# Inverse row sums of attention: written wide by VectorE and turned by four transposes a pair, in place of eight products of the identity

## The reference, cut to what matters

```python
p = exp(s - row_max(s))            # 512 x 512
o = (p @ v) / p.sum(axis=-1)       # 512 x 64: every row of o times the inverse of its row sum
```

## Time and profile before

| | |
|---|---|
| time before, median of 3 runs | 3227.48 us (3226.89 to 3227.84) |
| span of the profiled execution | 3226.3 us |
| its own time | not given apart from the span; the median of the runs is 1.2 us above the span, which is taken as what lies around it |
| TensorE products busy | 3183.2 us (99%) |
| VectorE busy | 1879.4 us (58%) |
| ScalarE, GpSimd busy | 512.8 us (16%), 231.0 us (7%) |
| attention of layer 1, 2621.80 to 2762.20 us: busy TensorE, VectorE, ScalarE | 129.89, 99.93, 82.37 us of 140.40 us |

### The profile page before, as it was taken

One profiled execution on the slowest core, in us unless ns is written; L12 is line 12 of the kernel. 1 busy time (PEld: TensorE's weight loads), 2 busy tenths in 40 slices (PEclk: granted clock), 3 DMA queues, 4 the chain that ended last, 5 costly groups with the idle time before them and its releaser, 6 DMA issues.

```text
span 3226.3 us, 36432 instructions
## 1 busy us (share of the span) xinstructions
PE 3183.2 (99%) x14382; PEld 2591.5 (80%) x14382; DVE 1879.4 (58%) x3268; ACT 512.8 (16%) x1080; POOL 231.0 (7%) x206
## 2 busy tenths in 40 slices
PE   9999999999999999999999999999999999999999
PEld 3888758888888888884488888888888854788888
DVE  6356845764347764464776664466644647766643
ACT  2111122000011000105521000110001145210001
POOL 1244400000000000003000000000000030000000
PEclk9999999999999999999999999999999999999999
DMA  5254321222222222223012222222222230122221
GB/s 237 89 173 161 135 70 53 92 80 90 92 82 92 82 85 85 90 72 124 1 64 81 92 86 88 89 83 87 88 85 88 74 124 1 53 92 88 82 84 61
DMA packets 43882, 288.31 MB, mean 89 GB/s; under 512 B 5404, under 2 KB 5404, under 8 KB 12736
## 3 DMA queue, kind: packets, MB, share of 16 engines
q1 hardware_dynamic: 39024, 271.14, 24.2%
q0 software_dynamic: 4688, 14.85, 1.4%
HBM read 281.76 MB, written 2.11 MB: 88 GB/s over the span
## 4 chain that ended last, share of the span: by engine, by line
PE 91%; DVE 5%; DVEq 1%; ACT 1%; issue 1%; DMA 0%; ACTq 0%; POOL 0%
PE ps L831 76%; PE ps L550 3%; PE ps L1274 2%; PE ps L966 1%; PE ps L1242 1%; PE ps L1185 1%; DVE arena L1888 1%; PE ps L531 1%; PE ps L858 1%; PE ps L931 1%; DVE arena L2310 1%; ACT arena L1586 1%; PE ps L1256 1%; DVEq L2323 1%; PE ps L1281 0%
## 5 line engine op out<-in xcount | busy, mean ns | idle before, releaser
L831 PE MATMUL ps<-arena 128*128 128x256 f32 x5456 | 1244.9, 379 | 0.1
L831 PEld LDWEIGHTS ps<-arena 128*128 128x128 f32 x5456 | 1036.6, 190 | 141.5 <-DVE arena L2061 0.5
L831 PE MATMUL ps<-arena,ring 128*128 128x256 f32 x2768 | 646.1, 379 | 0.5 <-ACT arena L1314 0.5
L831 PEld LDWEIGHTS ps<-arena,ring 128*128 128x128 f32 x2768 | 525.7, 190 | 72.4 <-ACT arena L1314 0.9
L831 PE MATMUL ps<-xn,ring 128*128 128x256 f32 x2272 | 518.8, 379 | 5.8 <-DVE arena L1704 2.3
L831 PEld LDWEIGHTS ps<-xn,ring 128*128 128x128 f32 x2272 | 431.2, 190 | 71.9 <-issue 9.4
L1698 DVE TENSOR_TENSOR arena<-arena,ps 128x512 f32<-128x512 f32 x173 | 118.9, 687 | 553.3 <-PE ps L831 494.4
L1671 DVE TENSOR_TENSOR arena<-ring 128x512 f32<-128x512 f32 (+1 forms) x194 | 131.1, 676 | 347.5 <-PE ps L831 347.3
L831 PE MATMUL ps<-xn,arena 128*128 128x256 f32 x1264 | 302.2, 379 | 0.0
L831 PEld LDWEIGHTS ps<-xn,arena 128*128 128x128 f32 x1264 | 240.2, 190 | 32.6
L1502 ACT ACTIVATE arena<-arena 128x512 f32<-128x512 f32 x88 | 55.4, 630 | 883.3 <-DVE arena L2180 883.3
(11 more groups left out here) (321 smaller groups left out, 2510.9 us busy)
## 6 DMA issues: line engine op xcount, KB each, us to landing
ring<-in_w_up_a SPq DMA_DIRECT2D x44, 1024.0 KB, 4.9
ring<-in_w_up_b SPq DMA_DIRECT2D x44, 1024.0 KB, 4.9
ring<-in_w_ff SPq DMA_DIRECT2D x32, 1024.0 KB, 4.9
ring<-in_w_ada SPq DMA_DIRECT2D x24, 1024.0 KB, 5.0
ring<-in_w_down_a SPq DMA_DIRECT2D x16, 1024.0 KB, 4.9
ring<-in_w_down_b SPq DMA_DIRECT2D x16, 1024.0 KB, 4.9
ring<-in_w_in SPq DMA_DIRECT2D x14, 1024.0 KB, 4.9
ring<-in_w_out SPq DMA_DIRECT2D x12, 1024.0 KB, 5.3
```

The lines of the kernel that those rows point to most:

```text
L831: mm = nc.tensor.matmul(out_ap, w, operand(product, quads[i]), start=at not in opened, stop=last_chunk and i == len(quads) - 1, skip_group ...
```

## The change

VectorE now follows the reciprocal with a drain (the copy reads what the reciprocal wrote) and a copy that repeats each of the eight inverses 64 times: `inv_wide`, 128 partitions x 512, in one of the two halves of a scratch buffer that is unused during attention. The semaphore `inverted` is raised by the copy. On TensorE the eight products with the identity (two passes each, 64 of the array's columns) become four 128 x 128 transposes of `inv_wide`, each giving the rows of both heads for one tile of queries.

```diff
+        inv_wide = square_of
...
                     for i in range(ST):
-                        for u in range(2):
-                            mm = nc.tensor.matmul(turn_bank((layer, "norm", j))[64 * u:64 * u + 64, i * P:(i + 1) * P],
-                                                  inv_p[:, j % 2, u, i:i + 1].to_broadcast([P, 64]), ident,
-                                                  start=True, stop=True)
+                        mm = nc.tensor.transpose(turn_bank((layer, "norm", j))[:, i * P:(i + 1) * P],
+                                                 inv_wide[:, j % 2, i * P:(i + 1) * P], ident)
                     mm.then_inc(sem("turned"), 1)
...
                 def invert(j, n):
                     dve.wait_ge(sem("exps"), UNITS_2 * layer + 2 * n + 2)
-                    nc.vector.reciprocal(inv_p[:, j % 2, :, :], sums_p[:, j % 2, :, :]).then_inc(sem("inverted"), 1)
+                    nc.vector.reciprocal(inv_p[:, j % 2, :, :], sums_p[:, j % 2, :, :])
+                    dve.drain()
+                    every = inv_p[:, j % 2, :, :].rearrange("p u (i o) -> p i u o", o=1).to_broadcast([P, ST, 2, 64])
+                    wide_to = inv_wide[:, j % 2, :].rearrange("p (i u w) -> p i u w", i=ST, u=2)
+                    nc.vector.tensor_copy(wide_to, every).then_inc(sem("inverted"), 1)
```

## The result

The changed kernel takes 3231.88 us (median of 21 runs, 3229.80 to 3233.37) against 3227.85 us for the kernel before (21 runs, 3226.75 to 3229.68): 4.0 us more, a ratio of 1.0013 with a 95% interval from 1.0007 to 1.0018. That is slower, by less than the 0.2% that was set as no change; the forecast was 3227.8, the range 3224.0 to 3233.0. So 1.9 us lie around a span, not the 1.2 taken before; the sum goes by differences, so that it does not enter.

A forecast was written before the change was run, and what follows sets the result against it. TensorE was taken to set the pace in long blocks, VectorE for some microseconds behind each. TensorE's -5.3 and VectorE's +5.6 gave +0.3 us on 3227.5, so 3227.8 us, range 3224.0 to 3233.0.

The forecast's parts named there:

- rival 1: VectorE's wide copy goes number by number because of its repeated source: +3.4 us, 3230.9 us; chance 0.22.
- rival 4: VectorE's wide copy waits for a full GpSimd add over shared SBUF ports: 7.4 us in all, 3235.2; chance 0.05.
- TensorE: what is removed and added: Transposes replacing identity products in attention save 2.63 us a layer, 5.3 in all, after paying for changes of tiling.
- A rule against the change: Skill's rule that TensorE transposes miss the full clock: new blocks 7.0 us longer in all, 3234.8; chance 0.02.
- VectorE: what is added: Drain and wide copy behind each reciprocal on VectorE add 0.49 us an invert, at the far end 0.75.
- What hides it: VectorE idle time hides the layer's first and last inverts; the others cost 2.81 us a layer, both 5.6.
- Rival 3: Longer VectorE work shifts TensorE's clock falls from C steps into B steps: two falls give 3234.6 us; chance 0.07.
- Rival 2: VectorE's additions behind the five on-chain reciprocals find cover: half covered 3225.0 us, all covered 3222.2; chance 0.12.

The follow-up runs named there:

- e1: Kernel before with only TensorE's side changed: four transposes of scratch data, no wide copy, so the turned numbers are not the inverses; 3221.33 us, ratio 0.9979.
- e3: Changed kernel with only the invert of each layer's first pair moved three steps later on VectorE's queue; 3228.89 us, ratio 1.0003 against the kernel before.
- e6: Changed kernel with the first pair's copy made a product reading one tile from SBUF, one from PSUM (that pair's result scaled wrongly); 3228.55 us, ratio 1.0003.
- e4: Changed kernel with all inverts but each layer's last moved three steps later on VectorE's queue; 3222.38 us, ratio 0.9983 against the kernel before.
- e2: Kernel before with only VectorE's side changed: drain and wide copy behind every reciprocal, identity products kept; 3236.60 us, ratio 1.0028.
- e5: Changed kernel run again, unedited, for a second trace; 3232.08 us, ratio 1.0014 against the kernel before.

## Why the prediction was right or wrong

The time lay in the upper part of the range, and within 0.2% as forecast; the sum missed by 3.7 us (+4.0 against +0.3). That it lay in the range is luck in part: the upper part was there for rival 1 and a fall of the clock, neither of which set the time. What did, rival 4, had been put beyond the range, at 3235.2. One sign of being right failed: the attention stretches were to keep their length within 1 us, and grew by 2.20 and 0.55 in the first trace, by 2.00 and 2.16 in the second.

- *TensorE: what is removed and added.* Right. Forecast 2.63 a layer; e1 has 2.68 and 2.62. Both halves of the price of a changed tiling, read from neighbouring rows, were there: 3.58 against 3.48 on leaving, 0.50 against 0.44 on arriving.
- *A rule against the change.* By the rule on transposes of the Trainium skill, "TensorE: Matmul & The Clock Gate", Part 4, the new block would have been 0.44 longer. It was not: four transposes and the way to the next group take 0.50 us in the rows above, with e1's 5.3 us of saving. The trace disagrees with the rule here. That transposes follow the granted clock shows where it fell: in the stretch at 0.51 of the earlier trace rows their step is 0.213 us, and 0.109 elsewhere.
- *VectorE: what is added.* Right in price: the copy stands 0.27 behind the reciprocal and is 427 ns long with its source repeated 64 times, so rival 1 falls. Forecast 2.81 a layer, measured (e3 less e1) 2.91 and 3.16; the larger one holds 0.17 more at C1, of which more below.
- *What hides it.* Here it failed, at A0: "hidden" rested on 1.03 us of idle time behind a copy of 0.34. The copy was 2.65 to 3.00 us long, 1.6 to 2.0 us more than the cover in A0's segment, in one layer of the first trace and in both of the second. That is 3.4 us in the second trace: -5.3 + 6.1 + 3.4 = +4.2, of the 4.3 measured.
- *Rival 4* was thus the case, with 0.05 for it. Its mechanism and its place at A0 were right, its price 1.3 a layer for A0 too small, and at B0 (2.4) nothing happened: the copy there is over before the add starts (1513.67 + 0.43 = 1514.10 against 1514.36 in the first trace). The step that failed is its "against", that the copies would start in a gap between adds. A copy has to end in it too. The 1688 ns that were read as agreeing are the middle of four times, two of 0.69 and two of 2.68 us. The Trainium skill, "SBUF — State Buffer", section on the two sides, has the pair of ports locked for a whole instruction by whichever starts first. The lock agrees with the long copies, which all end some 0.3 us behind the add; the order does not, as four of the five started 0.11 to 0.35 us ahead of it. e6 shows that the form of the operation decides. As to the gap: in the trace of before it runs at A0 from 1497.73 to 1498.27 and holds a DMA issue; the copy, put at 1498.07, would have ended at 1498.50, inside the add:

```profile
1497.69 0.56 POOL L732 DMA_DIRECT2D xn<-in_log_c  x1
```

- *Rival 3.* The granted clock fell in four C stretches for 3.4 us each in the first trace, at 1548.0 us for instance; no B stretch was hit. C3's segment in layer 1 is 26.07 us long in that trace and 26.07 in e3's, where a fall of 6.8 us lies in it (from 2719.8), so the falls did not set the time.
- *Rival 2* falls: no cover was found behind the five, B0's 0.41 to C1's 0.55 us are paid in full (layer 0, e3 against e1).

## What to carry to other kernels

An addition to an engine that is idle for 40% of the time can cost its full price, if it is queued where that engine is catching up; move it to where the engine waits, as e4 does, and it is free. Before a copy between SBUF tiles goes to VectorE, look at what GpSimd does at that moment and whether the copy ends before GpSimd's next add: e6's form, 0.69 us with a source in PSUM, was shorter here than a copy of 0.43 us that was held for 2.65 to 3.02. Rows of neighbouring operations priced TensorE's saving here to 0.05 us a layer, and VectorE's addition to 0.10 in layer 0 and 0.35 in layer 1; the term that failed had been costed at nothing.

## What was not expected

The copy is held by an add that starts after it: by 0.34 us in the first trace, 0.35 in e2's layer 1 (2635.10 against 2634.75), 0.11 and 0.14 in layer 0 of e2 and e5; only in e5's layer 1 does it start 0.02 us behind the add. Each time it ends 0.28 to 0.30 us behind the add's end. In the first four GpSimd was issuing a DMA when the copy started, which makes the issue a suspect. The rows speak against it. In the traces of the changed kernel, e2, e3 and e6, B0's copy starts some 0.1 us ahead of an issue, runs on into it and takes 0.43 us; no add starts before its end. And line 1884, in the trace of before an operation from SBUF to SBUF with one tile as its source, takes 0.54 us inside a row of eight issues, as it does alone, but up to 1.52 us beside an add (then it ends 0.3 us behind the add, as the copies do):

```profile
L1884 DVE TENSOR_SCALAR arena<-up_w,cols x8: 541/542/1524, 309.4 to 401.8; 128x512 f32<-128x512 f32 x8
...
401.76 0.54 DVE L1884 TENSOR_SCALAR arena<-up_w,cols 128x512 f32<-128x512 f32 x1
...
399.26 4.29 POOL L714 DMA_DIRECT2D arena<-cell_rows  x8 [24.84 <-DVE arena L1704]
```

All long copies have in common that less than their 0.43 us was left until the add. Why a copy that has started is held by an add that has not was not tried, and stays open.

In layer 1 of the changed kernel, and of e2, e3, e4 and e6, C1's segment is 0.35 us longer than in layer 0. The chain shows 0.43 us "issue" in VectorE's queue at 2684.37, where such a gap is otherwise 0.07:

```profile
2684.29 0.07 DVE other L2321
2684.37 0.43 issue
2684.79 0.22 DVE other L2323
```

Within these microseconds (2683 to 2686) the DMA queues moved a single packet, one of a queue marked as instruction. It starts at 2685.46, 0.67 us behind the end of the pause, so it is not what ended it. What VectorE waited for stays open.
